# Softmax normalisation of a band attention moved from the probabilities to the output of P V

## The chip, the core and the metric

The kernel runs on one core of a Trainium2 chip. The metric is the device time of one execution in microseconds. Times are those of the engines of that core: PE (TensorE, with its weight loads as PEld), DVE (VectorE), ACT (ScalarE), POOL (GpSimd) and SP (SyncE, which here only issues DMAs).

## The reference, cut to what matters

One residual block of 1024 tokens: a normalised input projection, band attention (8 heads of 64), a gated DeltaNet group, an output projection and a feed-forward part. The change lies in the attention group alone:

```python
scores = einsum('bcqhd,bckhd->bchqk', qc, kb) * Dh ** -0.5
scores = where(valid, scores + bias, -1e30)
p = softmax(scores, axis=-1)              # exp(s - max) / sum
out = einsum('bchqk,bckhd->bcqhd', p, vb)
```

Each token sees the keys of its own chunk of 64 and of the eight chunks before it, so a block of 128 queries sees at most five blocks of 128 keys. Dividing the exponentials by their sum before the product with V, or the product afterwards, gives the same output.

## The kernel before, in words

The attention stage works in 32 units. A unit is one pair of heads (4 pairs) and one block of 128 queries. Inside a pair the query blocks come in the order 0, 7, 1, 6, 2, 5, 3, 4, so the units 0 to 7 of a pair have 1, 5, 2, 5, 3, 5, 4, 5 key blocks. Units are counted from 0 to 31 below, so unit 9 is the second unit of the second pair. Each unit has two heads, s = 0 and 1.

A unit goes through these steps. There is no scheduler: every engine runs its list in the written order, and semaphores join the lists.

1. PE, `att_scores`, L1765: Q K into PSUM, for both heads in turn.
2. DVE, L1606, once a head: adds the bias tile, writes the sum to `SX` in SBUF and keeps the row's extreme in `neg_max` (two records in the trace, the second reads the accumulator).
3. ACT, `att_exp`, L890, once a head: the exponential in place in `SX`, with the row sum in `row_sum`.
4. DVE, L1620: the reciprocal of the two row sums, a 128x2 tile `row_inv`.
5. POOL, L786, once a head: multiplies the whole row of `SX` by its reciprocal, in place.
6. PE, `att_turn`, L1780: transposes up to four blocks of each head into PSUM. Where there is a fifth block (a tail), L1785 transposes those of both heads.
7. DVE, L1611, copies the four blocks of head 0 to `PT` in SBUF, ACT, L1098, those of head 1, and ACT, L1101, the two tail blocks.
8. PE, `att_pv`, L1797: P V into one 128x128 PSUM tile.
9. DVE, L1616: copies this tile to `PROJ`.

The lists are staggered. PE issues, for v = 0 to 31, the scores of unit v+2, the transposes of unit v and P V of unit v-1. The scores of unit v+2 wait until both bias additions of unit v+1 are done, since they reuse the PSUM of the scores. DVE issues in its round v the two bias additions of unit v, the copy of unit v-2, the output copy of unit v-3 and the reciprocal of unit v. ACT issues the two exponentials of unit v and the copies of unit v-2. POOL has only the multiplications, and behind them in its list the splitting of the output projection's weights (L286, L288); SP waits for these before it loads more weights (L279). After the last output copy the DeltaNet recurrence begins. In the first unit of each pair two memsets of the bias tile (L1600, L1601) come before DVE's additions.

Of the kernel before, what the change touches and what calls it, by code (L numbers as in the profile page):

```python
# [18 lines left out]
ALU = mybir.AluOpType  # L19
# [112 lines left out]
def hymba_block(nc, x, units, gain_mix, gain_q, gain_k, bias_rev, gain_att, conv_w, a_log, dt_bias,  # L132
                gain_dn, gain_ffn, w_gate, w_up, w_down, bias_ext, bias_rows, kept, hidden, down_t, gate_table, blocks, solved, pre, out):
    with ExitStack() as ctx:
# [20 lines left out]
        row_sum = sb("row_sum", [P, 2 * UNITS])  # L155
        row_inv = sb("row_inv", [P, 2 * UNITS])
        gain_att_col = sb("gain_att_col", [P, 4])
# [7 lines left out]
        def overlapped(*layouts):  # L165
            got = []
            for layout in layouts:
                with ExitStack() as stack:
# [16 lines left out]
        att_layout = [("BIAS", [P, 6, KEYS], F32),  # L185
                      ("SX", [P, 2 * UNITS, KEYS], F32), ("PT", [P, 2, 2 * KEYS], F32)]
        dn_one = ["PP", "WT", "VNEW", "OSQ", "ORS", "STATE"]
# [12 lines left out]
        ctx.enter_context(nc.sbuf_tensor("region1", [P, 2 * KT * T], F32))  # L200
        BIAS, SX, PT = att
        PP, WT, VNEW, OSQ, ORS, STATE, TT = dna[1:8]
# [150 lines left out]
        def add_rows(dve, t, bank):  # L353
# [8 lines left out]
        A = {n: sem("att_" + n) for n in  # L362
             ("gt_turned", "masked", "scores", "biased", "prob", "turned", "pt0", "pt1", "pv", "inv", "scaled", "ao",
              "sq", "sums", "ln", "rs", "mix")}
# [46 lines left out]
        def turned_count(v, part):  # L411
            return 2 * v + sum(map(tail, range(v))) + part + 1

        def copied_count(v, part):
            return v + sum(map(tail, range(v))) + part

# [63 lines left out]
        with nc.Block() as block:  # L480
# [254 lines left out]
            def _(pool):  # L735
# [46 lines left out]

                for v in range(NV):
                    pool.wait_ge(A["inv"], v + 1)
                    for s in range(2):
                        pool.tensor_scalar(sx(v, s), sx(v, s), stat(row_inv, v, s), None, ALU.mult).then_inc(A["scaled"], 1)  # L786
                for k in range(KT):
# [232 lines left out]
            def _(act):  # L1020
# [70 lines left out]
                for v in range(NV + 2):  # L1091
                    if v < NV:
                        for s in range(2):
                            att_exp(act, v, s)
                    if v >= 2:
                        w = v - 2
                        att_copy(act, w, 1)
                        act.activation(turned(w, 4, main(w)), ps_cols[:, turned_cols(w, 1)], ACT.Copy).then_inc(A["pt1"], 1)  # L1098
                        if tail(w):
                            att_copy(act, w, 2)  # L1100
                            act.activation(turned(w, 8, 2), ps_cols[:, 24 * P:26 * P], ACT.Copy).then_inc(A["pt1"], 1)  # L1101

# [403 lines left out]
            def _(dve):  # L1506
# [85 lines left out]
                for v in range(NV + 3):  # L1592
# [19 lines left out]
                    if v >= 3:  # L1612
                        w = v - 3
                        pair, qb, nt, kb0 = unit_of(w)
                        dve.wait_ge(A["pv"], w + 1)
                        dve.tensor_copy(PROJ[:, Q0 + pair, qb * P:(qb + 1) * P], ps_cols[:, PV_COLS]).then_inc(A["ao"], 1)  # L1616
                    if v < NV:
                        i = 2 * (v % UNITS)
                        dve.wait_ge(A["prob"], 2 * v + 2)
                        dve.reciprocal(row_inv[:, i:i + 2], row_sum[:, i:i + 2]).then_inc(A["inv"], 1)  # L1620

# [148 lines left out]
            def att_turn(pe, v):  # L1770
                for s in range(2):
                    pe.wait_ge(A["scaled"], 2 * v + s + 1)
                    if v >= 1:
# [4 lines left out]
                    for j in range(main(v)):  # L1778
                        first = turned_cols(v, s).start + j * P
                        mm = pe.transpose(ps_cols[:, first:first + P], sx(v, s)[:, j * P:(j + 1) * P], ident[:, :])  # L1780
                    mm.then_inc(A["turned"], 1)
                if tail(v):
                    ge(pe, A["pt1"], copied_count(v, 0))
                    for s in range(2):
                        mm = pe.transpose(ps_cols[:, (24 + s) * P:(25 + s) * P], sx(v, s)[:, 4 * P:5 * P], ident[:, :])  # L1785
                    mm.then_inc(A["turned"], 1)

# [368 lines left out]
```

## Time and profile before

| what | value |
|---|---|
| device time, median of 3 runs (lowest to highest) | 1469.29 us (1468.45 to 1470.76) |
| the profiled execution: its own time, its span | 1470.46 us, 1468.7 us |
| mean granted TensorE clock of that execution | 0.958 |
| busy: PE, PEld, DVE, ACT, POOL | 90%, 75%, 49%, 40%, 49% |
| the attention stage, first bias addition to last output copy | 460.49 to 569.63 us |

The page's row of POOL by slices, each a fortieth of the span (36.7 us), is `3322442322203987010301859788788787555542`; the 9, 8 and 7 in slices 14 to 16 are the attention stage. Elsewhere in the kernel the change touches no instruction.

### The profile page before, as it was taken

The page shows a single profiled execution, that of the slowest core. Times are in us where ns is not written, and L with a number is a line of the kernel's source. Part 1 is how long each engine was busy: PE and PEld are TensorE (multiplying, and loading weights), DVE is VectorE, ACT ScalarE, POOL GpSimd, SP SyncE. Part 2 cuts the span into 40 slices and gives each one's busy share as a digit, 9 for nine tenths or more (in the row PEclk, how much of TensorE's full clock was granted, in tenths as well). Part 3 has the DMA queues.
Part 4 walks back from the last instruction along what each step waited for, and adds up shares of the span by engine and source line. Part 5 has one row for each costly group of instructions (what it writes and reads, how often), then busy time and mean ns, then how long its engine had stood idle before and what let it go on. Part 6 is the DMA issues. An engine that isn't in the chain of part 4 may idle for free.

```text
span 1468.7 us, 18560 instructions
## 1 busy us (share of the span) xinstructions
PE 1320.0 (90%) x7000; PEld 1101.4 (75%) x7000; DVE 726.1 (49%) x1031; ACT 591.5 (40%) x953; POOL 714.3 (49%) x496
## 2 busy tenths in 40 slices
PE   5999998799924998777999859999999999999999
PEld 5888877688813776676887648888888888878887
DVE  5455543327102664434436846555555556634652
ACT  5578553452102665343323413333233333354441
POOL 3322442322203987010301859788788787555542
PEclk9999998899966999899999989999999999999999
DMA  6311353321004000322322033444444444787664
GB/s 244 116 43 58 101 158 111 90 72 43 20 7 146 30 2 29 138 78 72 115 101 74 27 105 146 165 165 165 165 165 165 165 165 165 269 297 220 195 191 153
DMA packets 73200, 181.41 MB, mean 124 GB/s; under 512 B 18120, under 2 KB 22288, under 8 KB 66072
## 3 DMA queue, kind: packets, MB, share of 16 engines
q1 hardware_dynamic: 71760, 176.52, 34.8%
q10 hardware_dynamic: 1352, 3.70, 0.7%
q8 instruction: 57, 0.93, 0.3%
q14 instruction: 31, 0.25, 0.1%
HBM read 128.49 MB, written 54.32 MB: 124 GB/s over the span
## 4 chain that ended last, share of the span: by engine, by line
PE 73%; DVE 6%; SPq 6%; DMA 5%; ACT 5%; issue 3%; POOL 2%; DVEq 0%; ACTq 0%
PE ps L1944 25%; PE ps L338 17%; PE ps L1969 11%; SPq L549 5%; PE ps L349 5%; PE ps L1765 2%; DMA KD<-pre 2%; PE ps L1797 2%; PE ps L1729 1%; PE ps L1857 1%; DMA RAB<-down_t 1%; POOL SX L786 1%; PE ps L1780 1%; PE ps L323 1%; PE ps L1746 1%
## 5 line engine op out<-in xcount | busy, mean ns | idle before, releaser
L338 PE MATMUL ps<-HT,SPLIT 128*128 128x512 f32 (+1 forms) x1488 | 331.8, 381 | 0.4 <-POOL SPLIT L288 0.4
L338 PEld LDWEIGHTS ps<-HT,SPLIT 128*128 128x128 f32 x1488 | 267.6, 191 | 50.9 <-issue 0.5
L1969 PE MATMUL ps<-S,HI 128*128 128x512 f32 x616 | 191.1, 391 | 2.5 <-POOL S L827 2.2
L827 POOL TENSOR_TENSOR S<-RAB,S 128x512 fp32r<-128x512 f32 x77 | 107.5, 1399 | 97.1 <-ACT S L1003 96.7
L286 POOL CAST SPLIT<-RAW 128x1024 fp32r<-128x1024 f32 x31 | 33.8, 1091 | 233.8 <-PE ps L338 228.5
L1969 PEld LDWEIGHTS ps<-S,HI 128*128 128x128 f32 x616 | 116.2, 189 | 27.7 <-issue 2.6
L786 POOL TENSOR_SCALAR SX<-SX,row_inv 128x640 f32<-128x640 f32 (+4 forms) x64 | 93.7, 1483 | 76.8 <-DVE row_inv L1620 76.6
L1944 PE MATMUL ps<-HI,WR 128*128 128x512 f32 x360 | 117.9, 397 | 7.5 <-ACT UV L968 3.9
L1944 PE MATMUL ps<-S,WR 128*128 128x512 f32 x516 | 121.0, 390 | 1.9 <-DVE S L1408 1.6
L1969 PE MATMUL ps<-S,LO 128*128 128x512 f32 x308 | 120.5, 391 | 0.0
L1944 PEld LDWEIGHTS ps<-S,WR 128*128 128x128 f32 x516 | 97.0, 188 | 23.0 <-issue 2.0
L1481 DVE TENSOR_TENSOR LO<-RAB,HI 128x512 fp32r<-128x512 f32 x77 | 65.4, 859 | 96.8 <-ACT HI L1000 96.8
L1944 PE MATMUL ps<-HI,WX 128*128 128x512 f32 x344 | 112.8, 389 | 0.2 <-DVE UV L1419 0.2
L1000 ACT ACTIVATE HI<-RAB 128x512 fp32r<-128x512 f32 x77 | 48.7, 633 | 111.4 <-PE ps L1969 63.6
L692 POOL TENSOR_TENSOR WR<-RAWG,WR 128x512 fp32r<-128x512 f32 x44 | 62.3, 1426 | 60.3 <-ACT WR L958 60.3
L1944 PEld LDWEIGHTS ps<-HI,WR 128*128 128x128 f32 x360 | 68.8, 191 | 23.5 <-issue 7.5
L1765 PE MATMUL ps<-PROJ 64*128 64x128 f32 x480 | 38.4, 302 | 49.0 <-DVE PROJ L1219 45.2
L1944 PE MATMUL ps<-S,WX 128*128 128x512 f32 x276 | 68.4, 398 | 12.7 <-ACT UV L973 11.7
L890 ACT ACTIVATE SX<-SX,neg_max 128x640 f32<-128x640 f32 (+4 forms) x64 | 44.0, 687 | 83.5 <-DVE neg_max L1606 83.5
L288 POOL TENSOR_TENSOR SPLIT<-RAW,SPLIT 128x1024 fp32r<-128x1024 f32 x31 | 75.2, 2424 | 2.5
L692 POOL TENSOR_TENSOR WR<-RAWU,WR 128x512 fp32r<-128x512 f32 x44 | 64.5, 1477 | 24.1 <-ACT WR L958 24.1
L286 POOL CAST WO<-RAW 128x1024 fp32r<-128x1024 f32 x6 | 8.2, 1371 | 138.0 <-DMA RAW<-units 138.0
(263 smaller groups left out, 2609.4 us busy)
## 6 DMA issues: line engine op xcount, KB each, us to landing
hidden<-HB SPq DMA_DIRECT2D x11, 1792.0 KB, 6.6
RAB<-hidden SPq DMA_DIRECT2D x77, 256.0 KB, 3.1
RAW<-units SPq DMA_DIRECT2D x37, 512.0 KB, 3.6
RAWG<-w_gate SPq DMA_DIRECT2D x11, 1024.0 KB, 10.8
RAWU<-w_up SPq DMA_DIRECT2D x11, 1024.0 KB, 5.0
RAWD<-w_down SPq DMA_DIRECT2D x11, 1024.0 KB, 8.8
down_t<-RAWD SPq DMA_DIRECT2D x11, 1024.0 KB, 3.8
RAB<-down_t SPq DMA_DIRECT2D x44, 256.0 KB, 3.5
```

Of the source, the lines that this page charges most:

```text
L288: pool.tensor_tensor(dst[:, 1, :], RAW[:, slot, :], dst[:, 0, :].bitcast(F32), ALU.subtract).then_inc(split_done, 1)
L338: mm = pe.matmul(ps[:, bank + a // HALF, a % HALF:a % HALF + width], w, right[other][:, k, a:a + width], start=(k == 0 and part == 0 and o ...
L349: mm = pe.matmul(ps[:, bank + dh, :], left(part), unit[:, other, dh * HALF:(dh + 1) * HALF], start=(first and part == 0 and other == 0), s ...
L549: sp.dma_start(solved[m, b * BLOCK:(b + 1) * BLOCK, h * P + b * BLOCK:h * P + (b + 1) * BLOCK], YB[first + b:first + b + 1, :, :]).then_in ...
L692: pool.tensor_tensor(weights(n)[:, 1, :], raw_block(u, RAW_AT[i]), weights(n)[:, 0, :].bitcast(F32), ALU.subtract).then_inc(F["lo"], 1)
L786: pool.tensor_scalar(sx(v, s), sx(v, s), stat(row_inv, v, s), None, ALU.mult).then_inc(A["scaled"], 1)
L827: pool.tensor_tensor(down_b(q, 1), RAB[:, q % RAWS, 1, :], down_b(q, 0).bitcast(F32), ALU.subtract).then_inc(R["b_lo"], 1)
L1000: act.activation(down_a(q, 0), RAB[:, q % RAWS, 0, :], ACT.Copy).then_inc(R["hi"], 1)
L1481: dve.tensor_tensor(down_a(q, 1), RAB[:, q % RAWS, 0, :], down_a(q, 0).bitcast(F32), ALU.subtract).then_inc(R["a_lo"], 1)
L1765: mm = pe.matmul(ps_cols[:, first:first + P], PROJ[rows, Q0 + pair, qb * P:(qb + 1) * P], PROJ[rows, K0 + pair, (kb0 + j) * P:(kb0 + j + 1 ...
L1944: mm = pe.matmul(ps[:, bank, :], weights(n)[:, part, k * P:(k + 1) * P], left_block(i, other, k), start=(i in (1, 5, 6, 7) and k == 0 and ...
L1969: mm = pe.matmul(ps[:, bank + t, :], down_a(q, part)[:, t * P:(t + 1) * P], down_b(q, other), start=(p == 0 and i in (1, 6, 5, 7) and part ...
```

## The change

The multiplications on POOL (L786) are gone, and the probabilities go unscaled through the transposes and the product. Instead:

- DVE writes the reciprocals 64 times over: one 128x128 tile `INVS` a unit, columns 0 to 63 for head 0 and 64 to 127 for head 1. There are four such tiles.
- PE transposes this tile once a unit, into one more block of PSUM (columns 26*P to 27*P), at the end of `att_turn`. In the result the row is the output channel (head and dimension) and the column the query, as in the P V tile.
- ACT copies this block to block 10 of `PT`: with a tail together with it, as one copy of three blocks in place of two, without a tail as a new copy of one block.
- DVE's output copy becomes a product of the P V tile in PSUM with that block.
- The waits change with it: the transposes wait for the exponential (`prob`), no longer for POOL (`scaled`); the new transpose waits for the reciprocal (`inv`); in units without a tail the wait for the second ACT copy of the unit before now stands ahead of the new transpose; ACT's last copy waits for the product of two units before (`ao`); the reciprocal waits for the new transpose of four units before (`turned`).

```diff
-                for v in range(NV):
-                    pool.wait_ge(A["inv"], v + 1)
-                    for s in range(2):
-                        pool.tensor_scalar(sx(v, s), sx(v, s), stat(row_inv, v, s), None, ALU.mult).then_inc(A["scaled"], 1)
...
-                        if tail(w):
-                            att_copy(act, w, 2)
-                            act.activation(turned(w, 8, 2), ps_cols[:, 24 * P:26 * P], ACT.Copy).then_inc(A["pt1"], 1)
+                        att_copy(act, w, 2)
+                        ge(act, A["ao"], w - 1 + AO0 if w >= 2 else 0)
+                        n = 3 if tail(w) else 1
+                        act.activation(turned(w, 11 - n, n), ps_cols[:, (27 - n) * P:27 * P], ACT.Copy).then_inc(A["pt1"], 1)
...
-                        dve.tensor_copy(PROJ[:, Q0 + pair, qb * P:(qb + 1) * P], ps_cols[:, PV_COLS]).then_inc(A["ao"], 1)
+                        dve.tensor_tensor(PROJ[:, Q0 + pair, qb * P:(qb + 1) * P], ps_cols[:, PV_COLS], turned(w, 10, 1),
+                                          ALU.mult).then_inc(A["ao"], 1)
...
-                        dve.reciprocal(row_inv[:, i:i + 2], row_sum[:, i:i + 2]).then_inc(A["inv"], 1)
+                        if v >= 4:
+                            dve.wait_ge(A["turned"], turned_count(v - 4, 2))
+                        dve.reciprocal(INVS[:, v % 4, :, :], row_sum[:, i:i + 2].unsqueeze(2).to_broadcast([P, 2, DHA])
+                                       ).then_inc(A["inv"], 1)
...
-                    pe.wait_ge(A["scaled"], 2 * v + s + 1)
+                    pe.wait_ge(A["prob"], 2 * v + s + 1)
...
+                ge(pe, A["pt1"], copied_count(v, 0))
                 if tail(v):
-                    ge(pe, A["pt1"], copied_count(v, 0))
                     for s in range(2):
-                        mm = pe.transpose(ps_cols[:, (24 + s) * P:(25 + s) * P], sx(v, s)[:, 4 * P:5 * P], ident[:, :])
-                    mm.then_inc(A["turned"], 1)
+                        pe.transpose(ps_cols[:, (24 + s) * P:(25 + s) * P], sx(v, s)[:, 4 * P:5 * P], ident[:, :])
+                pe.wait_ge(A["inv"], v + 1)
+                pe.transpose(ps_cols[:, 26 * P:27 * P], INVS[:, v % 4, :, :].rearrange("p s c -> p (s c)"), ident[:, :]
+                             ).then_inc(A["turned"], 1)
```

DVE's list in the round of the third unit of a pair (two key blocks), from its second bias addition to the start of the next round (five key blocks); `ISA` is the bias addition, and its `neg_max` row the read of the accumulator. Before:

```order
L1606 ISA SX,neg_max<-ps,BIAS 128x256 [waits att_turned,att_scores]
L1606 ISA neg_max 128x1
L1611 COPY PT<-ps 128x128 [waits att_pv,att_turned]
L1616 COPY PROJ<-ps 128x128 [waits att_pv]
L1620 RECIPROCAL row_inv<-row_sum 128x2 [waits att_prob]
L1606 ISA SX,neg_max<-ps,BIAS 128x640 [waits att_turned,att_scores]
```

Now:

```order
L1602 ISA SX,neg_max<-ps,BIAS 128x256 [waits att_turned,att_scores]
L1602 ISA neg_max 128x1
L1607 COPY PT<-ps 128x128 [waits att_pv,att_turned]
L1612 TENSOR_TENSOR PROJ<-ps,PT 128x128 [waits att_pv]
L1619 RECIPROCAL INVS<-row_sum 128x128 [waits att_turned,att_prob]
L1602 ISA SX,neg_max<-ps,BIAS 128x640 [waits att_turned,att_scores]
```

The order on DVE is the same: the reciprocal still stands between the exponentials of its own unit and the bias addition of the next, and has grown from two columns to 128.

ACT's list over three rounds (five, four and five key blocks, whose copies are those of two units before). Before:

```order
L890 ACTIVATE SX,row_sum<-SX,neg_max 128x640 [waits att_biased] x2
L1098 ACTIVATE PT<-ps 128x512 [waits att_pv,att_turned]
L1101 ACTIVATE PT<-ps 128x256 [waits att_pv,att_turned]
L890 ACTIVATE SX,row_sum<-SX,neg_max 128x512 [waits att_biased] x2
L1098 ACTIVATE PT<-ps 128x384 [waits att_pv,att_turned]
L890 ACTIVATE SX,row_sum<-SX,neg_max 128x640 [waits att_biased] x2
```

Now:

```order
L885 ACTIVATE SX,row_sum<-SX,neg_max 128x640 [waits att_biased] x2
L1093 ACTIVATE PT<-ps 128x512 [waits att_pv,att_turned]
L1097 ACTIVATE PT<-ps 128x384 [waits att_ao,att_pv,att_turned]
L885 ACTIVATE SX,row_sum<-SX,neg_max 128x512 [waits att_biased] x2
L1093 ACTIVATE PT<-ps 128x384 [waits att_pv,att_turned]
L1097 ACTIVATE PT<-ps 128x128 [waits att_ao,att_pv,att_turned]
L885 ACTIVATE SX,row_sum<-SX,neg_max 128x640 [waits att_biased] x2
```

Units with a tail have the same number of ACT copies, one of them longer; the others have one copy more. On PE each unit has one transpose more (L1787, `ps<-ident,INVS`), just ahead of P V of the unit before.

## Rows read from the trace of the kernel before

**Rows 1.** The page's costliest groups: POOL in the attention stage.
```profile
L786 POOL TENSOR_SCALAR SX<-SX,row_inv 128x640 f32<-128x640 f32 (+4 forms) x64 | 93.7, 1483 | 76.8 <-DVE row_inv L1620 76.6
```

**Rows 2.** Busy time by stretch, first and third pair of heads.
```profile
core 0: us, PE busy (x) PEld busy (x) DVE busy (x) ACT busy (x) POOL busy (x), PEclk, DMA share, GB/s
460.49:484.15 23.66, 20.90 (x220) 17.29 (x222) 14.21 (x49) 13.12 (x37) 18.13 (x13) 0.81 0.47 175
...
509.51:534.87 25.36, 24.83 (x304) 20.10 (x302) 17.21 (x59) 16.02 (x46) 23.42 (x17) 1.00 0.01 2
```

**Rows 3.** The chain that ended last, end of the stage: start us, us, what.
```profile
561.81 3.75 POOL SX L786 x2
...
565.61 0.65 PE ps L1780 x4
```

**Rows 4.** Timeline of DVE: start us, us, line, operation; one period of eight units.
```profile
511.14 0.29 DVE L1606 CUSTOM_DVE_ANT_0 SX<-ps,BIAS 128x128 f32<-128x128 f32 x1
...
514.42 0.82 DVE L1606 CUSTOM_DVE_ANT_0 SX<-ps,BIAS 128x640 f32<-128x640 f32 x1 [0.94 <-PE ps L1765]
...
517.06 0.17 DVE L1620 RECIPROCAL row_inv<-row_sum 128x2 f32<-128x2 f32 x1
517.47 0.42 DVE L1606 CUSTOM_DVE_ANT_0 SX<-ps,BIAS 128x256 f32<-128x256 f32 x1 [0.25 <-PE ps L1765]
...
520.54 0.82 DVE L1606 CUSTOM_DVE_ANT_0 SX<-ps,BIAS 128x640 f32<-128x640 f32 x1 [0.93 <-PE ps L1765]
...
523.29 0.56 DVE L1606 CUSTOM_DVE_ANT_0 SX<-ps,BIAS 128x384 f32<-128x384 f32 x1
...
529.81 0.69 DVE L1606 CUSTOM_DVE_ANT_0 SX<-ps,BIAS 128x512 f32<-128x512 f32 x1 [0.25 <-PE ps L1765]
```

**Rows 5.** Timeline of ACT in the same period.
```profile
509.51 0.81 ACT L890 ACTIVATE SX<-SX,neg_max 128x640 f32<-128x640 f32 x1
...
510.32 0.57 ACT L1098 ACTIVATE PT<-ps 128x512 f32<-128x512 f32 x1
...
512.17 0.19 ACT L890 ACTIVATION_READ_ACCUMULATOR SX<-SX,neg_max 128x1 f32 x1
...
515.29 0.83 ACT L890 ACTIVATE SX<-SX,neg_max 128x640 f32<-128x640 f32 x1 [2.45 <-DVE neg_max L1606]
...
516.12 0.81 ACT L890 ACTIVATE SX<-SX,neg_max 128x640 f32<-128x640 f32 x1
...
517.41 0.37 ACT L1101 ACTIVATE PT<-ps 128x256 f32<-128x256 f32 x1
...
518.84 0.19 ACT L890 ACTIVATION_READ_ACCUMULATOR SX<-SX,neg_max 128x1 f32 x1
...
525.01 0.19 ACT L890 ACTIVATION_READ_ACCUMULATOR SX<-SX,neg_max 128x1 f32 x1
...
531.88 0.19 ACT L890 ACTIVATION_READ_ACCUMULATOR SX<-SX,neg_max 128x1 f32 x1
531.98 0.47 ACT L1098 ACTIVATE PT<-ps 128x384 f32<-128x384 f32 x1
```

**Rows 6.** The reciprocals of two widths: duration ns min/median/max.
```profile
L1620 DVE RECIPROCAL row_inv<-row_sum x32: 153/166/168, 461.7 to 561.2; 128x2 f32<-128x2 f32 x32
...
L1535 DVE RECIPROCAL beta<-beta x1: 353/353/353, 58.7 to 58.7; 128x32 f32<-128x32 f32 x1
```

**Rows 7.** Timeline of PE in the same period.
```profile
511.18 0.66 PE L1780 MATMUL ps<-ident,SX 128*128 128x128 f32 x4 [0.33 <-ACT PT L1101]
511.76 1.31 PE L1797 MATMUL ps<-PT,PROJ 128*64 128x128 f32 x20
513.00 1.39 PE L1765 MATMUL ps<-PROJ 64*128 64x128 f32 x20
```

**Rows 8.** Products on DVE with one operand in PSUM: ns min/median/max.
```profile
L1433 DVE TENSOR_TENSOR HB<-ps,UV x22: 678/684/693, 856.7 to 1249.3; 128x512 f32<-128x512 f32 x22
```

**Rows 9.** Timeline of DVE, the last output copy of the stage.
```profile
569.34 0.29 DVE L1616 COPY PROJ<-ps 128x128 f32<-128x128 f32 x1 [1.50 <-PE ps L1797]
```

More of the change, by code:

```diff
@@ L155, in hymba_block @@
         row_sum = sb("row_sum", [P, 2 * UNITS])
-        row_inv = sb("row_inv", [P, 2 * UNITS])
         gain_att_col = sb("gain_att_col", [P, 4])
@@ L185, in hymba_block @@
         att_layout = [("BIAS", [P, 6, KEYS], F32),
-                      ("SX", [P, 2 * UNITS, KEYS], F32), ("PT", [P, 2, 2 * KEYS], F32)]
+                      ("SX", [P, 2 * UNITS, KEYS], F32), ("PT", [P, 2, 2 * KEYS + P], F32), ("INVS", [P, 4, 2, DHA], F32)]
         dn_one = ["PP", "WT", "VNEW", "OSQ", "ORS", "STATE"]
@@ L200, in hymba_block @@
         ctx.enter_context(nc.sbuf_tensor("region1", [P, 2 * KT * T], F32))
-        BIAS, SX, PT = att
+        BIAS, SX, PT, INVS = att
         PP, WT, VNEW, OSQ, ORS, STATE, TT = dna[1:8]
@@ L362, in hymba_block @@
         A = {n: sem("att_" + n) for n in
-             ("gt_turned", "masked", "scores", "biased", "prob", "turned", "pt0", "pt1", "pv", "inv", "scaled", "ao",
+             ("gt_turned", "masked", "scores", "biased", "prob", "turned", "pt0", "pt1", "pv", "inv", "ao",
               "sq", "sums", "ln", "rs", "mix")}
@@ L411, in turned_count @@
         def turned_count(v, part):
-            return 2 * v + sum(map(tail, range(v))) + part + 1
+            return 3 * v + part + 1
         def copied_count(v, part):
-            return v + sum(map(tail, range(v))) + part
+            return 2 * v + part
         def sx(v, s):
```

## The prediction

> **What bounds the kernel now.** I read the page's costliest groups first. The reader is to see that POOL spends 93.7 us on the 64 multiplications that go [rows 1], in a stage that lasts 109.14 us (460.49 to 569.63; its end is the end of the last output copy, 569.34 + 0.29 [rows 9]). By busy time POOL looks like the limit, so the second view is the busy time by stretch. From the second pair of heads on the stage repeats itself every 25.36 us. In such a period POOL is busy for 23.42 us, but PE for 24.83, at a granted clock of 1.00, the 2.4 GHz level [rows 2]. Two engines are nearly full, and taking work from one of them gains only what the other leaves.
>
> The third view, the chain that ended last, shows where POOL does end last: it carries the end of the stage, up to the transposes of the last unit at 565.61 [rows 3]. The timelines show the loops that run beside it. PE's scores of unit v+2 release DVE's bias addition, this ACT's exponentials, behind them stands ACT's copy of unit v, and this releases the transposes of unit v+1, P V of unit v, and then the scores of unit v+4. I call it the long loop. The short loop has no PE in it: bias addition of v, two exponentials, reciprocal of v, bias addition of v+1. Before, the short loop has slack: the reciprocal at 517.06 is followed by a bias addition only at 517.47, released by PE [rows 4].
>
> **What the change costs, step by step.**
>
> *POOL's 64 multiplications go.* What they hold up in a period is little, because PE waits for ACT's copy at the same place. Transposes of unit 14 for head 1 start at 511.18 [rows 7], while ACT's copy was ready at 510.32 + 0.57 = 510.89 [rows 5], so with the 0.05 of a handover at 510.94: 0.24 us a period. At the end of the stage it is more, worked out below.
>
> *The reciprocal grows from 128x2 to 128x128.* The trace has no such operation, but two widths: 128x2 takes 0.166 us (median) and 128x32 takes 0.353 [rows 6]. That is (353 - 166) / 30 = 6.23 ns a column, and 353 + 96 x 6.23 = 951 ns for 128. An ordinary DVE operation costs far less, (0.82 - 0.29) / 512 = 1.04 ns a column [rows 4]. The two ends for 128 columns: below, 0.353 + 96 x 1.04 = 0.45 us, if the further columns ran at the rate of ordinary operations; above, 4 x 0.353 = 1.41 us, if the 128x32 row had no fixed part at all. I take 0.95, the straight line through the rows. That is 32 x 0.79 = 25 us more of DVE, whose share of a period rises from 17.2 to 23.5 us.
>
> The Trainium skill, "VectorE: DVE Perf Modes", section "First, the fixed hardware budget", says that Reciprocal is an iterative divide with a repeat count of 8. Eight cycles of the 0.96 GHz it gives would be 8.3 ns a column, an estimate of 1.2 us for 128 columns; the trace's two widths differ by 6.2 ns a column and so disagree with that reading, and I go by the trace.
>
> *What this does to the short loop.* Its length for a unit runs from the start of a bias addition to the end of the exponentials, plus 0.03 to the reciprocal and 0.91 for it (0.95, of which the next instruction overlaps 0.04).
> - five blocks: 517.06 - 514.42 = 2.64, + 0.91 = 3.55
> - four: 531.88 + 0.19 + 0.03 - 529.81 = 2.29, + 0.91 = 3.20
> - three: 525.01 + 0.22 - 523.29 = 1.94, + 0.91 = 2.85
> - two: 518.84 + 0.22 - 517.47 = 1.59, + 0.91 = 2.50
> - one: 512.17 + 0.22 - 511.14 = 1.25, + 0.91 = 2.16 [rows 4, 5]
>
> A period has four units of five blocks and one of each other: 14.2 + 3.20 + 2.85 + 2.50 + 2.16 = 24.9, with the two memsets at the start of a pair (511.14 against 509.51 + 0.94 + 0.12 = 510.57, where the addition could have begun) about 25.4 us. Before, the same sum is 8 x 0.79 shorter, 19.1. So the short loop alone now takes as long as the whole period did.
>
> *PE gets 32 transposes and ACT 16 copies more.* Four transposes fill the 0.58 us from 511.18 to 511.76 [rows 7], 0.15 us each. I take 0.20 for one that stands alone with its waits. The new wait of PE for `inv` costs nothing: the scores of v+2, ahead of it in PE's list, already wait for a bias addition that stands behind this reciprocal. The wait moved ahead in units without a tail is one that P V had anyway, so only the transpose itself follows it. ACT's longer copy takes 0.47 in place of 0.37 [rows 5]. The output product instead of the copy costs nothing: a product from PSUM takes 0.684 for 512 columns [rows 8], so 0.684 - 384 x 1.04 ns = 0.29 for 128, as the copy [rows 9]. ACT's wait for `ao` and DVE's for `turned` name work of two and four units before and are long met.
>
> *The period.* I follow it from unit 7's second exponential (509.51 is that of unit 15) to the same place eight units later.
> - First the long loop: 509.51 to 514.42 was 4.91; less 0.24 for POOL, plus 0.20 for the new transpose: 4.87.
> - Long loop again, 514.42 to 520.54: 6.12, plus 0.10 for ACT's longer copy and 0.20 for the transpose: 6.42.
> - Then the short loop through four units (five, three, five, four blocks) and into the fifth: 3.55 + 2.85 + 3.55 + 3.20 and 1.70 from bias addition to second exponential (516.12 - 514.42), 14.85. Before, the rest of the period was 25.36 - 4.91 - 6.12 = 14.33.
>
> Sum 26.14 against 25.36: +0.8 us a period. From pair 1 to pair 3 there are two such periods: +1.6. The last pair has the first two stretches (+0.26) and then the end. The first pair (23.66 us to its last exponential, at a granted clock of 0.81 [rows 2], with PE between 1.2 and 2.4 GHz) is limited by slow scores for its first three units; from there on it has the same 14.85 for 14.33, which is +0.5, and I choose 0.2 more for those three units: +0.7.
>
> *The end of the stage.* Before, from bias addition 27 to the end: 14.33 + (569.63 - 560.23) = 23.73, with POOL ending last. After: 14.85, then 1.43 to the transposes (510.94 - 509.51), 0.58, the new transpose 0.20, P V 1.24 (513.00 - 511.76), the transposes of the last unit for head 0 0.58, and from those for head 1 at 565.61 on [rows 3] the 4.02 us that were there, plus 0.15 for the last new transpose: 23.05. So -0.7.
>
> Sum: 0.7 + 1.6 + 0.3 - 0.7 = +1.9 us. The own time of the profiled execution was 1470.46, 1.76 over its span of 1468.7 and 1.2 over the median. Its spans stand for all runs, so I add the 1.9 to the median: 1469.3 + 1.9 = **1471.2 us**.
>
> *What moves along.* POOL's splitting of two output units no longer stands behind the multiplications and ends some 70 us earlier; SP's next two loads go out then. Nothing waits for them before the output projection. The recurrence starts when the stage ends and shifts with it.
>
> **The rivals.**
>
> *A. The reciprocal is the whole limit (slower).* At 1.2 us, halfway between the line and the upper end, the short loop takes 25.4 + 8 x 0.25 = 27.4 us, longer than the path through PE, and every unit lies on it: +2.0 a period, about +8 over four pairs, less 0.7 at the end: 1476.6. For it: a column costs six times that of other operations, from two widths only, and the operand is now a broadcast. Against: the two widths fit a line with a fixed part of 0.15 us. It decides from about 1.0 us on.
>
> *B. The added transposes cost more (slower).* If each costs 0.3 to 0.4 with its wait instead of 0.2, two of them lie in the long loop's part of a period, and a third is late enough to count: +0.5 a period, 4 x 0.5 on top of the forecast, 1473.2. For it: PE is busy 24.83 of 25.36. Against: four transposes in 0.58 us. The Trainium skill, "TensorE: Matmul & The Clock Gate", section "Part 4: PE-mode transpose", gives about 275 ns for one 128x128 transpose in a kernel; the trace's spacing is half of that, and by the page's figure this rival would be the forecast.
>
> *C. POOL was the limit (faster).* If the reciprocal's columns come at the ordinary rate, 0.45 us, the short loop falls to 21.4 us and drops out. The period then is 25.4 at best, since PE keeps its work and gets more; only the end gains: after 560.23 it is 1.43 + 0.58 + 0.20 + 1.24 + 0.58 + 4.17 = 8.2 instead of 9.4. That is -1.2, and with 0.3 to 0.6 a period that PE no longer loses to POOL, up to -3.5: 1465.8 to 1468.1. For it: POOL's 92% in a period. Against: the 6.2 ns a column.
>
> *D. Everything stays under cover (same).* The loops take turns differently and the period stays 25.4: 1468.5 to 1469.5.
>
> **How the numbers follow.** Forecast case 0.50 (its own range 1469.5 to 1473), A 0.13, B 0.15, C 0.08, D 0.14. 0.2% is 2.9 us, about what a measurement of this kernel tells from no change. Slower by more than that: all of A, most of B and a fifth of the forecast case, 0.34. Faster: most of C, 0.07. Same: the rest, 0.59. The range goes from the middle of C to the foot of A: 1466.8 to 1476.5.
>
> **What would show it right or wrong.** Right: the reciprocal's rows near 0.95 us; a period of 26.1 us between same units of two pairs; in the second half of a pair bias additions that follow the reciprocal with no idle time, and PE idle ahead of scores, released by DVE; POOL idle, and the last pair's end shorter by about 0.7. Wrong: a reciprocal under 0.6 or over 1.1 us; a period under 25.4; transposes of `INVS` before which PE waits for DVE; or a difference that lies outside the stage.

## The result: slower by 0.29%, and the profile after

| what | value |
|---|---|
| before, median of 20 runs | 1468.66 us (1465.09 to 1472.22) |
| changed, median of 20 runs | 1473.19 us (1469.53 to 1479.69, and one of 1736.63) |
| ratio, 95% interval | 1.0029 (1.0018 to 1.0040) |
| the profiled execution of the changed kernel: its own time, its span | 1471.0 us, 1469.3 us |

The one run of 1736.63 us is outside the ratio, which is taken between undisturbed runs.

The busy time by stretch, one period of eight units of the changed kernel (columns as in [rows 2], of which the second row is the period before):

```profile
core 0: us, PE busy (x) PEld busy (x) DVE busy (x) ACT busy (x) POOL busy (x), PEclk, DMA share, GB/s
510.29:536.24 25.95, 25.53 (x310) 21.09 (x310) 23.15 (x60) 17.11 (x48) 0.00 (x0) 1.00 0.01 2
```

POOL went from 23.42 us to nothing, and the period grew from 25.36 to 25.95. PE has 0.70 us more, DVE 5.9, ACT 1.1. The groups of the new operations, from the views of their lines (duration ns min/median/max):

```profile
L1619 DVE RECIPROCAL INVS<-row_sum x32: 941/953/954, 462.1 to 564.8; 128x128 f32<-128x128 f32 x32
...
L1612 DVE TENSOR_TENSOR PROJ<-ps,PT x32: 280/291/292, 473.6 to 571.5; 128x128 f32<-128x128 f32 x32
...
L1787 PE MATMUL ps<-ident,INVS x32: 272/273/421, 467.3 to 568.4; 128*128 128x128 f32 x32
```

The reciprocal is the 166 and 353 ns of [rows 6] carried on to 128 columns: 953 ns. The output product takes what the copy took. The timeline of DVE at the last unit of the first pair and the third unit of the second, to be laid beside [rows 4]:

```profile
483.47 0.95 DVE L1619 RECIPROCAL INVS<-row_sum 128x128 f32<-128x128 f32 x1 [0.23 <-ACT SX L885]
484.35 0.76 DVE L1602 CUSTOM_DVE_ANT_0 SX<-ps,BIAS 128x640 f32<-128x640 f32 x1
...
493.47 0.95 DVE L1619 RECIPROCAL INVS<-row_sum 128x128 f32<-128x128 f32 x1
494.33 0.36 DVE L1602 CUSTOM_DVE_ANT_0 SX<-ps,BIAS 128x256 f32<-128x256 f32 x1
```

From the fifth unit of the stage on no bias addition waits for PE any more; each follows the reciprocal at once (at the start of a pair, the memsets behind it). That looks like a stage bound by the short loop of DVE and ACT. The chain that ended last in the same kernel says something else (start us, us, what):

```profile
514.19 1.24 PE ps L1799 x20
515.43 1.31 PE ps L1765 x20
516.75 1.02 PE ps L1780 x8
517.77 0.22 PE ps L1785 x2
517.99 0.11 PE ps L1787
518.10 1.02 PE ps L1799 x16
519.12 0.65 PE ps L1765 x8
```

PE goes from product to scores to transposes without a gap, and the new transpose (L1787) is a link of 0.11 us in that chain. In the whole period the chain leaves PE for longer than 0.12 us only once, between 523.2 and 526.4, for a bias addition, its copies and ACT; no reciprocal stands in it. Which of the two readings holds is what the experiments had to say.

For all comparisons I use one ruler: the start of the first bias addition of units 0, 7, 15, 23 and 31 and the end of the last output copy. The timeline of DVE in the kernel before, at units 7 and 15, between which the first period of 25.35 us lies:

```profile
482.46 0.82 DVE L1606 CUSTOM_DVE_ANT_0 SX<-ps,BIAS 128x640 f32<-128x640 f32 x1 [0.91 <-PE ps L1765]
507.81 0.82 DVE L1606 CUSTOM_DVE_ANT_0 SX<-ps,BIAS 128x640 f32<-128x640 f32 x1 [0.91 <-PE ps L1765]
```

And the same ruler in the changed kernel, its DVE timeline from unit 0 to the last product:

```profile
460.91 0.29 DVE L1602 CUSTOM_DVE_ANT_0 SX<-ps,BIAS 128x128 f32<-128x128 f32 x1
...
510.29 0.76 DVE L1602 CUSTOM_DVE_ANT_0 SX<-ps,BIAS 128x640 f32<-128x640 f32 x1
...
536.24 0.76 DVE L1602 CUSTOM_DVE_ANT_0 SX<-ps,BIAS 128x640 f32<-128x640 f32 x1
562.18 0.76 DVE L1602 CUSTOM_DVE_ANT_0 SX<-ps,BIAS 128x640 f32<-128x640 f32 x1
...
571.54 0.29 DVE L1612 TENSOR_TENSOR PROJ<-ps,PT 128x128 f32<-128x128 f32 x1 [1.50 <-PE ps L1799]
```

Every kernel, in us by this ruler, each from one trace:

| kernel | unit 0 to 7 | period | unit 31 to end | stage | ratio of time (95%) |
|---|---|---|---|---|---|
| before | 21.97 | 25.36 | 11.10 | 109.14 | 1 |
| before, second trace | 22.09 | 25.35 | 11.10 | 109.32 | 0.9997 (0.9983 to 1.0011) |
| changed | 23.44 | 25.95 | 9.65 | 110.92 | 1.0029 (1.0018 to 1.0040) |
| changed, second trace | 23.58 | 25.95 | 9.64 | 111.06 | 1.0023 (1.0010 to 1.0036) |
| changed, POOL spreads | 21.88 | 25.91 | 9.70 | 109.32 | 1.0004 (0.9993 to 1.0016) |
| before, wide reciprocal | 23.33 | 26.75 | 11.51 | 115.08 | 1.0040 (1.0025 to 1.0055) |
| no scaling | 22.21 | 25.11 | 9.49 | 107.04 | 0.9992 (0.9979 to 1.0006) |
| no scaling, wide reciprocal | 22.81 | 25.31 | 9.42 | 108.17 | 0.9995 (0.9983 to 1.0007) |
| no scaling, transposes | 21.85 | 25.71 | 9.71 | 108.70 | 0.9996 (0.9985 to 1.0008) |
| changed, two transposes | 23.77 | 26.46 | 9.93 | 113.07 | 1.0018 (1.0006 to 1.0029) |
| changed, splits held | 23.16 | 25.95 | 9.65 | 110.65 | 1.0025 (1.0012 to 1.0037) |
| before, DVE scales six | 22.30 | 25.20 | 13.33 | 111.23 | 1.0000 (0.9988 to 1.0013) |
| the same, splits held | 21.79 | 25.20 | 9.49 | 106.88 | 0.9987 (0.9978 to 0.9997) |
| the same, second trace | 21.78 | 25.20 | 9.49 | 106.87 | 0.9992 (0.9977 to 1.0006) |

The three kernels without scaling leave the division by the row sums out, so they compute something else; they are there to price single terms. The column of the period is read from the two later pairs. It repeats within 0.02 us between pairs and between traces, but for one pair of the second trace of before that is 0.08 longer, so differences of 0.1 us in it can be read, where the device time has an interval of up to 2 us to either side. The column of the first seven units is rougher: the changed kernel has 23.44, 23.58 and, with the splits held, which touches nothing there, 23.16.

The prediction cut a period into three stretches: from the second exponential of unit 15 to the first bias addition of unit 17, from there to that of unit 19, and from there to the second exponential of unit 23. The same three, in us, from the timelines of DVE and ACT:

| kernel | first | second | third | sum |
|---|---|---|---|---|
| before | 4.91 | 6.12 | 14.33 | 25.36 |
| forecast | 4.87 | 6.42 | 14.85 | 26.14 |
| changed | 4.86 | 6.43 | 14.66 | 25.95 |
| changed, POOL spreads | 4.85 | 6.43 | 14.63 | 25.91 |
| no scaling | 4.75 | 6.11 | 14.25 | 25.11 |
| no scaling, wide reciprocal | 4.75 | 6.12 | 14.45 | 25.32 |
| no scaling, transposes | 4.86 | 6.32 | 14.53 | 25.71 |

### The profile page after: what moved, and what is told of

Its sections match the earlier page's. It is cut to its first block, busy times and chain, and to the rows that moved or that the text cites. A ratio compares the mean times of both kernels' runs of the same rounds, so it can differ in the third digit from the quotient of the medians.

```text
span 1469.3 us, 18634 instructions
## 1 busy us (share of the span) xinstructions
PE 1320.8 (90%) x7032; PEld 1105.2 (75%) x7032; DVE 752.3 (51%) x1031; ACT 595.9 (41%) x969; POOL 622.1 (42%) x432
## 4 chain that ended last, share of the span: by engine, by line
PE 74%; SPq 6%; DVE 6%; DMA 5%; ACT 4%; issue 3%; POOL 1%; DVEq 0%; ACTq 0%
PE ps L1946 25%; PE ps L337 17%; PE ps L1971 11%; SPq L548 5%; PE ps L348 5%; PE ps L1765 2%; PE ps L1799 2%; DMA KD<-pre 2%; PE ps L1780 2%; PE ps L1729 1%; PE ps L1859 1%; PE ps L322 1%; DMA RAB<-down_t 1%; SPq L557 1%; PE ps L1746 1%
## 5 line engine op out<-in xcount | busy, mean ns | idle before, releaser
L1971 PE MATMUL ps<-S,HI 128*128 128x512 f32 x616 | 189.8, 389 | 1.4 <-POOL S L822 1.4
L1971 PEld LDWEIGHTS ps<-S,HI 128*128 128x128 f32 x616 | 115.6, 188 | 25.8 <-issue 1.8
L1971 PE MATMUL ps<-S,LO 128*128 128x512 f32 x308 | 119.8, 389 | 0.0
L1946 PEld LDWEIGHTS ps<-HI,WX 128*128 128x128 f32 x344 | 64.6, 188 | 13.9 <-issue 0.5
```

What stands on the lines that cost most here:

```text
L1946: mm = pe.matmul(ps[:, bank, :], weights(n)[:, part, k * P:(k + 1) * P], left_block(i, other, k), start=(i in (1, 5, 6, 7) and k == 0 and ...
L1971: mm = pe.matmul(ps[:, bank + t, :], down_a(q, part)[:, t * P:(t + 1) * P], down_b(q, other), start=(p == 0 and i in (1, 6, 5, 7) and part ...
```

## The experiments

**Is it the reciprocal? POOL spreads it.**

```diff
+                for v in range(NV):
+                    i = 2 * (v % UNITS)
+                    pool.wait_ge(A["inv"], v + 1)
...
+                    pool.tensor_copy(INVS[:, v % 4, :, :], row_inv[:, i:i + 2].unsqueeze(2).to_broadcast([P, 2, DHA])
+                                     ).then_inc(A["spread"], 1)
...
-                        dve.reciprocal(INVS[:, v % 4, :, :], row_sum[:, i:i + 2].unsqueeze(2).to_broadcast([P, 2, DHA])
-                                       ).then_inc(A["inv"], 1)
+                        dve.reciprocal(row_inv[:, i:i + 2], row_sum[:, i:i + 2]).then_inc(A["inv"], 1)
...
-                pe.wait_ge(A["inv"], v + 1)
+                pe.wait_ge(A["spread"], v + 1)
```

> The changed kernel, but DVE takes the reciprocals of two columns as before and the idle POOL spreads them over the 128 columns of INVS. Theory S (the long reciprocal sets the short loop of DVE and ACT, PE's added transposes cost little by themselves): the period of eight units goes from 25.95 us in the changed kernel to 25.4 to 25.8, the stage ends about 2 us earlier than in the changed kernel, near its end before the change; time within 2 us of before. Rival P (the added transposes and copies alone carry the loss): the period stays at 25.9 to 26.1, the time stays 3 to 4 us over before. Rival Q (POOL had been the limit): the period falls under 25.2 and the kernel is 3 us or more faster than before.

The period stayed: 25.91. The stage nevertheless lost 1.6 us, all of it in the first seven units (23.44 to 21.88), and the time came back to that of before. Its bias additions wait for PE again, as before the change (the timeline of DVE, the first bias additions of units 15 and 23, where the period begins and ends):

```profile
507.98 0.82 DVE L1610 CUSTOM_DVE_ANT_0 SX<-ps,BIAS 128x640 f32<-128x640 f32 x1 [0.94 <-PE ps L1770]
...
533.89 0.82 DVE L1610 CUSTOM_DVE_ANT_0 SX<-ps,BIAS 128x640 f32<-128x640 f32 x1 [0.94 <-PE ps L1770]
```

So in the repeated part the way through PE takes 25.91 us without the long reciprocal, and taking 0.8 us a unit from the short loop of DVE and ACT gives 0.04 us. Rival P was right on the period, theory S on the time.

**The reciprocal alone in the kernel before.**

```diff
-                        pool.tensor_scalar(sx(v, s), sx(v, s), stat(row_inv, v, s), None, ALU.mult).then_inc(A["scaled"], 1)
+                        pool.tensor_scalar(sx(v, s), sx(v, s), INVS[:, v % 4, s, 0:1], None, ALU.mult).then_inc(A["scaled"], 1)
...
-                        dve.reciprocal(row_inv[:, i:i + 2], row_sum[:, i:i + 2]).then_inc(A["inv"], 1)
+                        dve.reciprocal(INVS[:, v % 4, :, :], row_sum[:, i:i + 2].unsqueeze(2).to_broadcast([P, 2, DHA])
+                                       ).then_inc(A["inv"], 1)
```

> The kernel before, with only the reciprocal made 128 columns wide; POOL still scales, with one column of each head. Theory S: the short loop takes 25.4 us and the long way through POOL and PE adds to it, so the period goes from 25.36 to 26 to 27 us and the time up by 3 to 7 us, more than the whole change cost. Rival P (DVE has slack, the reciprocal is hidden): period 25.4 and no change of time.

Period 26.75, stage 115.08, time up by 0.4%, as theory S expected. With POOL behind it the reciprocal delays the scaling and through it PE: what PE's weight loads wait for POOL grows from 1.0 us a period before to 3.0. As expected, the reciprocal alone costs more than the whole change, since the change takes away what stood behind it.

**What POOL's work had cost at most: no scaling at all.**

```diff
-                for v in range(NV):
-                    pool.wait_ge(A["inv"], v + 1)
-                    for s in range(2):
-                        pool.tensor_scalar(sx(v, s), sx(v, s), stat(row_inv, v, s), None, ALU.mult).then_inc(A["scaled"], 1)
...
-                    pe.wait_ge(A["scaled"], 2 * v + s + 1)
+                    pe.wait_ge(A["prob"], 2 * v + s + 1)
```

> Leaves the division by the row sums out: the kernel before without POOL's multiplications, nothing put in their place (the reciprocal of two columns stays). It gives the most that taking the work off POOL can bring. Theory S: PE and the long loop stay, the period is 24.7 to 25.1 us (25.36 less the waits for POOL), the end of the stage gains 1 to 3 us, in all 3 to 5 us faster. Rival Q (POOL was the limit of the stage): the period falls to 24 us or less, 6 us or more faster.

Period 25.11, the end 1.6 us shorter, the stage 2.1 us shorter, near what theory S expected. The 3 to 5 us of device time that it expected did not come: the ratio of 0.9992 can't be told from 1. POOL was 92% busy and its removal is worth 1% of the period. The busy time by stretch of this kernel, one period:

```profile
core 0: us, PE busy (x) PEld busy (x) DVE busy (x) ACT busy (x) POOL busy (x), PEclk, DMA share, GB/s
509.41:534.53 25.12, 24.50 (x301) 20.14 (x302) 17.25 (x59) 16.02 (x44) 0.00 (x0) 1.00 0.01 2
```

PE is busy for 24.50 of 25.12 us with nothing from POOL to wait for.

**The short loop nearly bare: no scaling, wide reciprocal.** The edit is that of the run without scaling, and the reciprocal's of the second experiment.

> As the run without scaling, but with the reciprocal 128 columns wide (its result goes unused); the division is left out here too, and no transposes or copies are added. Theory S: the short loop of 25.4 us shows nearly bare, period 25.4 to 25.7, that is 0.6 to 0.8 us a period more than without it, time within 1.5 us of before. Rival P (the added transposes carry the loss, the reciprocal is hidden): period as in the run without scaling, 24.7 to 25.1, and 3 to 5 us faster than before.

Period 25.31, only 0.2 us over the run without scaling, where theory S had 0.6 to 0.8 and a period of 25.4 to 25.7: both missed. Here the bias additions follow the reciprocal without idle time, so this is the short loop bare. It is 0.6 us a period shorter than the way through PE with the added transposes and copies (25.91, in the first experiment).

**PE's share: 32 transposes alone.**

```diff
                 if tail(v):
                     ge(pe, A["pt1"], copied_count(v, 0))
+                    pe.transpose(ps_cols[:, 26 * P:27 * P], sx(v, 0)[:, 0:P], ident[:, :])
...
+                if not tail(v):
+                    ge(pe, A["pt1"], copied_count(v, 0))
+                    pe.transpose(ps_cols[:, 26 * P:27 * P], sx(v, 0)[:, 0:P], ident[:, :])
```

> The run without scaling plus 32 transposes, one a unit at the place and with the waits of the changed kernel; their result is not read, and the division is left out. Period 25.11 us without them, 25.91 with transposes, copies on ACT and product. Theory P2 (PE's work is what counts): 25.6 to 25.9, nearly all of the 0.8. Rival (ACT's copies carry it): 25.1 to 25.4.

These transposes do not wait for the reciprocal, and in units with a tail they stand ahead of the two tail transposes and not behind them. Period 25.71, inside theory P2's range: of the 0.80 us between no scaling (25.11) and the full change with a cheap reciprocal (25.91), the eight transposes carry 0.60 and the copies and the product 0.20. The share of the three stretches is 0.11, 0.21 and 0.28. The busy time by stretch, the same pair in this kernel:

```profile
core 0: us, PE busy (x) PEld busy (x) DVE busy (x) ACT busy (x) POOL busy (x), PEclk, DMA share, GB/s
510.00:535.71 25.71, 25.33 (x309) 21.09 (x310) 17.29 (x59) 16.01 (x44) 0.00 (x0) 1.00 0.01 2
```

**And the transposes doubled** in the changed kernel, the line of the transpose written twice.

> The changed kernel with the transpose of INVS issued twice a unit, the same output. Theory P2 (after the first four runs: past the first pair PE is full, and every transpose added lies on the path): 0.11 to 0.13 us a unit more, the period goes from 25.95 to 26.8 to 27.0 us, the stage grows by 3 to 4 us. Theory S as first stated (the short loop of DVE and ACT holds half of each period): only the transposes in the long loop count, the period grows by 0.2 to 0.4 us.

Period 26.46: +0.51, between the two expectations, so both missed. In the timeline of PE the second transpose of a unit starts 0.11 us after the first, eight of them are 0.88 us, and somewhat over half of that shows. PE is near its limit, not at it. The stage is 3.9 us over before, the time only 0.18%, 2.6 us.

**A version with less PE work: the kernel before, DVE scales six.** DVE does head 1 of the seventh unit of each pair, head 1 of unit 29 and both heads of unit 31, just behind the reciprocal; `ext_filled` is a semaphore that is free by then.

```diff
+        def by_dve(v, s):
+            return (v % NT == 6 and s == 1) or (v in (29, 30) and s == 1) or v == 31
...
+                        for s in range(2):
+                            if by_dve(v, s):
+                                dve.wait_ge(A["inv"], v + 1)
+                                dve.tensor_scalar(sx(v, s), sx(v, s), stat(row_inv, v, s), None, ALU.mult).then_inc(ext_filled, 1)
```

> The kernel before, with six of the 64 multiplications taken from POOL and done by DVE just behind the reciprocal: head 1 of the seventh unit of each pair (the one whose transposes waited for POOL), head 1 of unit 29 and both heads of unit 31. No work is added to PE. If POOL costs the stage only those waits and its lag at the end: period 25.1 us as in the run without scaling, the end 1 to 1.6 us shorter, the stage 2 us shorter than before, time 0 to 3 us under before. If DVE's operation holds up its next bias addition: period 25.4 or more and no gain.

The period was near what was hoped, 25.20, but the end grew to 13.33 us. The timelines of DVE and POOL there:

```profile
561.05 3.97 DVE L1633 TENSOR_SCALAR SX<-SX,row_inv 128x640 f32<-128x640 f32 x2
...
561.09 1.04 POOL L286 CAST SPLIT<-RAW 128x1024 fp32r<-128x1024 f32 x1 [1.58 <-DVE row_inv L1629]
...
562.21 2.47 POOL L288 TENSOR_TENSOR SPLIT<-RAW,SPLIT 128x1024 fp32r<-128x1024 f32 x1
```

POOL, done earlier with its multiplications, had moved on to splitting the output weights, and DVE's two multiplications took 3.97 us beside it. PE waited for them, and then did its last work at a lower granted clock, 0.56 of full speed from 567 to 569 us and 0.68 from 569 to 571.6. So the splitting was held back:

```diff
                     if k == 0:
                         pool.wait_ge(unit_used, U_OUT)
+                        pool.wait_ge(A["ao"], NPAIR * NT + AO0)
```

> As the run in which DVE does six of the multiplications, but POOL's splitting of the output projection's weights is held until the last output copy. In that run the last two multiplications on DVE took 3.97 us together beside POOL's splitting, against 0.5 us each elsewhere, and the end of the stage came 2.2 us late. Theory L (the two engines shut each other out of something they share): the two take about 0.5 us each, the end of the stage shrinks from 13.33 to 9.4 to 10 us, the period stays 25.2, the stage is 107.5 to 108 us, time 0 to 3 us under before. Rival (the product of unit 31 is slow for another reason): the end stays over 12 us.

The timeline of DVE in this version, its last multiplications and an output copy:

```profile
561.08 1.02 DVE L1634 TENSOR_SCALAR SX<-SX,row_inv 128x640 f32<-128x640 f32 x2
...
567.44 0.29 DVE L1626 COPY PROJ<-ps 128x128 f32<-128x128 f32 x1 [1.50 <-PE ps L1812]
```

The two took 1.02 us, the end 9.49, the stage 106.88: 2.3 us under before, and less than the 107.5 to 108 expected. That it is shorter than even the run without scaling lies in the first seven units alone (21.79 against 22.21), which scatter by as much; the periods are 25.20 and 25.11, the ends both 9.49. Once more, because the interval nearly reached 1:

> The version in which DVE does six multiplications and POOL's splitting is held, once more, since its first ratio of 0.9987 came with an interval that nearly touches 1. Its stage was 106.9 us against 109.1 to 109.3 before, which is 2.3 us or 0.16%: the stage again 106.9 us, ratio 0.998 to 1.0. A ratio of 1 or more would make the first one scatter.

The stage again 106.87 us, ratio 0.9992 (0.9977 to 1.0006). The stage is surely shorter; that the kernel is faster by about 0.1% is likely, and a single comparison of this length can't tell it from nothing.

**What lies behind the stage.** Three runs ask why the time grew by more than the stage. The changed kernel once more:

> The changed kernel once more, for a second trace and its time on the chip of the other runs. The first timing gave a ratio of 1.0029, the stage only 1.8 us (0.12%). If the rest is something the change does behind the stage, the parts behind the stage are again 1 to 2 us longer than before in this trace; if it is scatter of the clock's half-speed windows, the parts behind the stage differ either way and the ratio comes out nearer 1.0015.

The kernel before against itself:

> The kernel before once more, against itself, for a second trace. It shows what a ratio of no change scatters by, and whether the DeltaNet part of 149.9 us and the start of the stage at 460.5 us belong to the kernel or to one execution. If the changed kernel is slower behind the stage for good, this trace has 149.9 us again; if it is scatter, it lies anywhere from 149 to 151. Ratio within 0.15% of 1.

And the changed kernel with the splitting held, by the same edit as above:

> The changed kernel, with POOL's splitting of the first two output units held until the last output product, so that SP's two loads behind it go out at the end of the stage as before the change. If the early splits and loads cost time behind or inside the stage, the time falls by 1 to 3 us against the changed kernel; if not, stage 110.9 us and the same time as the changed kernel, within 1.5 us.

The second ratio of the changed kernel is 1.0023, that with the splits held 1.0025: the early splitting is not the cause.

The DeltaNet part, from the end of the stage to the start of its last product on DVE (L1309 in the kernel before), took 151.0 and 150.9 us in the traces of the changed kernel, 150.1 and 150.5 in those of before, 150.7 with the splits held, 148.0 and 148.6 in the two traces of the last version. No kernel changes an instruction of this part. All fourteen traces lie between 148.0 and 151.8, and two traces of one kernel differ by up to 0.6 us, so the 0.4 to 0.9 in question is within the spread between kernels.

From the end of the stage to the end of the span the two traces of before took 899.1 and 898.2 us, those of the changed kernel 897.5 and 897.9, and that with the splits held 900.9. So behind the stage the traces of the changed kernel are not longer than those of before. What they do have is stretches in which the granted clock of TensorE falls to the 1.2 GHz level, and these fall differently from one execution to the next. From 1299 to 1303 us the granted clock of the first trace of before is 0.57, that of the changed kernel 1.00; the last part, from the first product of L1969 (L1971 in the changed kernel) to the end of the span, took 217.5 us in the one and 214.6 in the other.

## Why the prediction was right, point by point

**The sum.** Forecast +1.9 us, range 1466.8 to 1476.5; measured +4.5 (1.0029), inside the range, but just outside the 1469.5 to 1473 that I had given the forecast case. By class I gave "same" 0.59 and "slower" 0.34; slower by over 0.2% is what came. In the stage, where all my terms lie, the trace has +1.78 us (110.92 - 109.14) and the second pair of traces +1.74. That this is so near +1.9 is in part luck, since the terms miss in both directions:

| term | forecast | measured |
|---|---|---|
| first pair, to its last exponential | +0.7 | +1.41 (23.66 to 25.07) |
| two periods | +1.6 | +1.18 (25.36 to 25.95 each) |
| last pair, to bias addition 27 | +0.26 | +0.26 (11.02 to 11.28) |
| from there to the end | -0.7 | -1.06 (23.74 to 22.68) |

Of the +4.5 us of device time 1.8 are in the stage. For the rest I had no term.

**The reciprocal.** Forecast 0.95, measured 0.953. The straight line through two widths held at four times the wider of them. The reading of the Trainium skill, "VectorE: DVE Perf Modes", "First, the fixed hardware budget", that I set beside it (a repeat count of 8, taken as eight cycles a column, an estimate of 1.2 us) does not hold in the trace: 6.2 ns a column. With it rival A falls, which needed about 1.0 us or more.

**The period.** Forecast 26.14, measured 25.95. The first two stretches came within 0.01 us. The step that failed is the third: I gave it 14.85 us for the short loop alone and left the way through PE out there. Bare, in the run without scaling and with the wide reciprocal, the short loop takes 14.45 us in this stretch, 0.40 less than I had added up. (Around a whole period it measures 25.31 against my 25.4, and that was luck too: my own terms, 24.9 and 0.57 for the memsets, give 25.5.) PE's way through the same stretch, with the cheap reciprocal, takes 14.63, and the changed kernel has 14.66. So a loop taken 0.40 too long stood in for a path that I had not counted. In place of it: with POOL's waits gone the way through PE is the longer one, and 0.60 of the 0.80 us that is then added comes from eight transposes, at 0.075 us each. I had counted two of them, at 0.20 each; those two stretches measure 0.32, and the other six of the eight add 0.28 in the third. Rival B, dearer transposes, named the right engine for the wrong reason: they are not dear, there are eight of them on the path and not two. A record of one lasts 273 ns, but the next starts 0.11 us after it.

Of the signs that I had named, the bias additions that follow the reciprocal with no idle time came, and were no proof of the short loop: they stand beside a busy PE just as well. The other half of that sign failed. PE was to idle ahead of scores, released by DVE, and in the period that wait is 0.2 us in all, with PE busy for 25.53 of 25.95.

**The first pair.** Forecast +0.7, measured +1.4 (and +1.5 by the ruler above). The first three units take 0.57 more, where I had 0.2, and the rest 0.84, where I had 0.5. The chain that ended last, in the first pair of the changed kernel:

```profile
464.87 1.74 ACT SX L885 x4
466.61 0.02 issue
466.63 0.95 DVE INVS L1619
...
468.27 2.50 PE ps L1765 x20
470.78 1.90 PE ps L1780 x8
472.68 0.43 PE ps L1785 x2
```

One reciprocal stands in it, and from 468.27 on to the end of the pair it does not leave PE. The transposes from 470.78 on run at a lower clock: from 470 to 475 us the granted clock is 0.70, in the first trace of before 1.00. The reciprocal begins the loss, since 1.56 us go when POOL spreads it; but the trace in which it does has 1.00 from 470 on as well, and without the transposes the wide reciprocal adds only 0.60 (22.21 to 22.81). The late rise of the clock is not the change's alone: the second trace of before has 0.75 there and loses 0.12. So the short loop was not the limit of the last five units as I had it, and how the 1.4 us divide among reciprocal, transposes and clock stays open.

**The end.** From bias addition 27 on, forecast -0.7, measured -1.06. Up to the second exponential of unit 31 it is +0.33, where I had +0.5 for the short loop; behind it -1.39 (9.40 to 8.01), where I had -1.2. POOL's lag at the end, seen in [rows 3], was worth 1.6 us in the run without scaling.

**POOL's waits** in the period: taken 0.24, measured 25.36 - 25.11 = 0.25, but not where I had put it: 0.16 in the first stretch, 0.01 in the second, 0.08 in the third. I had taken 0.05 for the handover from ACT's copy to the transposes. In the run without scaling that copy ends at 512.49 and the transposes start at 512.64. The same 0.15 after 510.89 in the kernel before leaves 0.14 for POOL. In the first stretch this error and the 0.20 for a transpose that measures 0.11 cancel.

The waits that the change adds (`inv`, `ao`, `turned`) cost nothing seen: no row of waits names DVE ahead of the transpose of `INVS`. The wait that it moves ahead of that transpose, for ACT's copy, shows with 0.5 us in three places of the whole stage. Rivals C and D fall: nothing was gained, and the period did move.

**Left open.** The device time grew by 3.4 to 4.5 us in the two timings and the stage by 1.8. The lower ends of the intervals, 1.5 and 2.6 us, leave little beyond the stage, and the version with two transposes, which has all of the change and a longer stage still, grew by 2.6 us alone. But three timings of the changed kernel, one with the splits held, agree on 0.23 to 0.29%. A difference outside the stage was a sign of being wrong that I had named; whether there is one the runs don't settle, and no trace shows where it would be.

## What to carry to other kernels

Before an engine that is 92% busy is relieved, add up the engines beside it: here PE had 0.25 us of waiting in a period to give back, and every replacement added work to PE or to the loop of DVE and ACT that was nearly as long (25.3 of 25.9 us). When two paths are nearly equal, undoing the cost of the shorter one shows nothing in the steady part, so read the chain as well as the idle times, and take away each suspect by itself. And an engine that is freed starts its next work earlier; look at what that work collides with.

## What the runs showed of the hardware that I had not expected

DVE's reciprocal costs 6.2 ns a column of 128 partitions, six times the 1.04 of its bias additions, in a straight line from 2 to 128 columns (0.166, 0.353, 0.953 us). Replicating a value by taking its reciprocal 64 times over is dear for that reason: POOL's spreading copies did the same in 2.35 us a period, where DVE is busy for 5.9 us more in the changed kernel (23.15 against 17.30).

DVE's multiplications and POOL's operations shut each other out. DVE's multiplication of 128x640 from SBUF to SBUF takes 0.55 us, faster than its bias addition of the same size from PSUM (0.82), but the two that met POOL's weight splitting took 3.97 us together, 1.02 without it. The slowest single one took 2.63 us (the view of DVE's multiplication line in the kernel where DVE scales six, its splits not held; ns min/median/max):

```profile
L1633 DVE TENSOR_SCALAR SX<-SX,row_inv x7: 485/486/2632, 481.7 to 562.4; 128x512 f32<-128x512 f32 x4, 128x640 f32<-128x640 f32 x3
```

It works the other way too: beside DVE's multiplication one of POOL's takes 2.24 us instead of 1.88. The timeline of POOL in the version with the splits held:

```profile
554.72 2.24 POOL L795 TENSOR_SCALAR SX<-SX,row_inv 128x640 f32<-128x640 f32 x1
```

DVE's own multiplication starts there at 554.66 and takes 0.55.

The Trainium skill, "SBUF — State Buffer", section "Who interferes with whom", says that only the port pair shared by the two engines causes contention, and that it is an exclusive lock. The traces agree as far as they show it: DVE's second slow multiplication starts at 562.4, POOL's instruction beside it runs from 562.21 to 564.68, and the multiplication ends 0.3 us after that. DVE's operations with a PSUM operand kept their durations beside POOL: a bias addition of 128x640 takes 0.82 us in the kernel before, with POOL 92% busy, and in the run without scaling, with POOL idle.
